# A tenth 2 MB home for expert weights, and half of each gather moved behind the pair's first unit

## The reference, cut to what matters

```
x = x + mixed @ w_out
h = rmsnorm(x, ln2)
logits = h @ w_router + b_router
top_v, top_i = top_k(logits, 4)            # 4 of 32 experts
gate = softmax(top_v)
for each expert e and its tokens:
    gu = h @ w_gate_up[e] + b_gate_up[e]   # 1024 x 2048
    gt, up = gu[:, :1024], gu[:, 1024:]
    gt = minimum(gt, 7); up = clip(up, -7, 7)
    y = ((up + 1) * gt * sigmoid(1.702 * gt)) @ w_down[e] + b_down[e]   # 1024 x 1024
    x = x + gate * y
y_prompt, y_sample = rmsnorm(x, ln_f)
```

## Time and profile before

| | |
|---|---|
| median of three runs | 1280.0 us (1279.75 to 1284.23) |
| the profiled execution | 1278.74 us, its span 1276.9 us |
| PE busy | 1204.8 us, 94% of the span |
| DVE, ACT, POOL busy | 27%, 16%, 7% |
| DMA | 458.76 MB, mean 359 GB/s |
| unit loads | 192 of 2 MB, 36 to 40 us from issue to landing |
| expert loop | 351.2 to 1266.1 us |

### The profile page before, as it was taken

How to read it: one execution, slowest core, us unless ns; L and a number is a source line. 1 busy time by engine, 2 the same in 40 slices (tenths; PEclk the granted TensorE clock), 3 DMA queues, 4 the chain that set the end, 5 groups by cost and what they waited for, 6 DMA issues and landing times.

```text
span 1276.9 us, 18583 instructions
## 1 busy us (share of the span) xinstructions
PE 1204.8 (94%) x7592; PEld 590.1 (46%) x7592; DVE 339.3 (27%) x655; ACT 208.3 (16%) x421; POOL 87.0 (7%) x64
## 2 busy tenths in 40 slices
PE   6999999999999999999998989999898989898997
PEld 5877789875543433434333333324242433333332
DVE  1068497566411111111111111011111111111102
ACT  3133253320310110111011001000110101010002
POOL 0161003711000000000000000000000000000001
PEclk9999999999999999999999999999999999999999
DMA  9879450158699999999999999999999999999994
GB/s 318 196 249 300 141 210 12 37 191 339 272 379 428 428 427 429 428 426 428 428 429 425 429 428 427 427 428 429 427 428 428 428 428 428 427 428 427 428 427 185
DMA packets 52656, 458.76 MB, mean 359 GB/s; under 512 B 7092, under 2 KB 10844, under 8 KB 28004
## 3 DMA queue, kind: packets, MB, share of 16 engines
q1 hardware_dynamic: 49972, 452.22, 86.2%
q0 software_dynamic: 1824, 5.12, 1.7%
q10 hardware_dynamic: 784, 0.28, 0.1%
HBM read 453.74 MB, written 3.82 MB: 358 GB/s over the span
## 4 chain that ended last, share of the span: by engine, by line
PE 60%; DMA 29%; DVE 6%; ACT 2%; POOL 1%; issue 1%; SPq 0%; DVEq 0%; ACTq 0%; POOLq 0%
DMA ring<-in_w_gate_up 29%; PE ps L1902 24%; PE ps L1409 8%; PE ps L1923 7%; PE ps L1835 6%; PE ps L1882 3%; PE ps L1740 2%; PE ps L1844 2%; DVE work L904 2%; PE ps L1911 1%; DVE ring L904 1%; PE ps L1385 1%; PE ps L1727 1%; DVE ring L949 1%; PE ps L1657 1%
## 5 line engine op out<-in xcount | busy, mean ns | idle before, releaser
L1902 PE MATMUL ps<-ring,work 128*64 128x512 f32 x1456 | 326.5, 596 | 32.8 <-DMA ring<-in_w_gate_up 30.8
L1902 PEld LDWEIGHTS ps<-ring,work 128*64 128x64 f32 x1456 | 100.9, 137 | 236.9 <-issue 190.7
L1299 DVE TENSOR_SCALAR work<-ps 128x512 f32<-128x512 f32 x32 | 22.1, 692 | 529.0 <-PE ps L1902 529.0
L1409 PE MATMUL ps<-work,ring 128*128 128x264 f32 x672 | 156.4, 392 | 2.3 <-ACT work L552 2.2
L1902 PE MATMUL ps<-work 128*64 128x512 f32 x592 | 132.7, 594 | 11.6 <-DMA work<-in_w_gate_up 11.6
L1409 PEld LDWEIGHTS ps<-work,ring 128*128 128x128 f32 x672 | 127.5, 192 | 28.1 <-issue 6.2
L1923 PE MATMUL ps<-ring,work 128*64 128x512 f32 x608 | 137.3, 597 | 0.0
L1923 PE MATMUL ps<-work 128*64 128x512 f32 x416 | 93.3, 593 | 0.6 <-DMA work<-in_w_down 0.6
L1317 DVE SCALAR_TENSOR_TENSOR work<-work 128x512 f32<-128x512 f32 x32 | 24.0, 752 | 240.9 <-ACT work L775 240.9
L1902 PEld LDWEIGHTS ps<-work 128*64 128x64 f32 x592 | 42.4, 137 | 95.2 <-issue 88.9
L1923 PEld LDWEIGHTS ps<-ring,work 128*64 128x64 f32 x608 | 41.2, 137 | 92.7 <-issue 90.5
(11 more groups left out here) (276 smaller groups left out, 889.8 us busy)
## 6 DMA issues: line engine op xcount, KB each, us to landing
ring<-in_w_gate_up SPq DMA_DIRECT2D x91, 2048.0 KB, 36.3
ring<-in_w_down SPq DMA_DIRECT2D x38, 2048.0 KB, 40.1
work<-in_w_gate_up SPq DMA_DIRECT2D x37, 2048.0 KB, 36.8
work<-in_w_down SPq DMA_DIRECT2D x26, 2048.0 KB, 39.2
ring<-in_w_in SPq DMA_DIRECT2D x5, 3072.0 KB, 16.4
ring<-in_w_out SPq DMA_DIRECT2D x1, 4096.0 KB, 14.1
ring<-in_w_in SPq DMA_DIRECT2D x2, 1536.0 KB, 9.0
ring<-in_cache_k SPq DMA_DIRECT2D x16, 192.0 KB, 7.5
```

What stands on the lines that cost most here:

```text
L1299: v.tensor_scalar(gt, PS[BG][:, :], LIMIT, None, ALU.min).then_inc(S_("gt"), 1)
L1409: last_ = mm(psum(job, T), w, hT[:, k, :], start=k == 0, stop=k == KD - 1)
L1902: last = mm(PS[bnk][g * 64:g * 64 + 64, :], lhs, UNIT[n % 9][:, w0 + base + g * 512:w0 + base + (g + 1) * 512], start=False, stop=k == KD - 1)
```

## The change

1. **Ten homes.** `HOMES` is 10; a home of 4096 columns at `WORK` 520 joins. It lies over constants that only the first part needs, over small tensors and old state. So the constants are re-ordered, the ones needed late first; two of them are stored narrower, and `before` is loaded later, next to the router, at another place. `acc` moves to `WORK` 4616, small late tensors to 17352.
2. **Releases.** Units 3 and 4 are released at the fourth step of the `mb` products (behind the wait for `obT` 4), units 5 and 6 after `mb7` ahead of the sample's output projection, 7 and 8 after `wo10` and `wo11`, 9 with `open_sum(1, 1)`.
3. **Residual input.** It is loaded into `h2`, by POOL, after `obT` 4 and after all seven stores of `st_out`, the state's among them. `residual` adds PSUM and `h2` into `acc`.
4. **One `XG`.** `gather(0)` of the next pair moves from behind `combine` to k = 4 of the second expert, and `gather(1)` of the pair itself comes at k = 2 of its first expert, into bank BY. `act_T` moves to k = 2 of the second expert. DVE builds the next `sel` after that `gather(1)`.
5. **Small loads.** `ebias` is laid out over 128 partitions and loaded after `ht21`; `ln_f` is loaded by SP behind the last unit, when unit 182 has been used.
6. **Loops.** PE's loop holds all 16 pairs, SP's five pairs a turn. Some semaphores are merged.

```diff
-        UNIT = [view(RING, 4096 * 5, 4096), view(RING, 4096 * 2, 4096), view(RING, 4096 * 3, 4096), view(RING, 4096 * 4, 4096),
-                view(WORK, 13256, 4096), view(WORK, 24504, 4096), view(RING, 0, 4096), view(RING, 4096, 4096),
-                view(WORK, 2792, 4096)]
+        UNIT = [view(RING, 4096 * 5, 4096), view(RING, 4096 * 2, 4096), view(RING, 4096 * 3, 4096), view(WORK, KEPT, 4096),
+                view(WORK, 13256, 4096), view(RING, 4096 * 4, 4096), view(WORK, 24504, 4096), view(RING, 0, 4096),
+                view(RING, 4096, 4096), view(WORK, 4616, 4096)]
...
-            for m in range(2):
-                load(acc[:, m, :], A["x_prompt"][0, m * 128:(m + 1) * 128, :], "ld_acc")
-            load(acc[:NB, 2, :], A["x_sample"][:, 0, :], "ld_acc")
...
+            sp.wait_ge(S_("unit_used"), sp.snap(passes * (6 * NE) + (HOMES + 183 - 6 * NE)))
+            load(lnfb, A["ln_f"].unsqueeze(0).broadcast_to([128, D]), "ld_lnf")
...
+            pool.wait_ge(S_("obT"), 4)
+            pool.wait_ge(S_("st_out"), 16 * 7)
+            for m in range(2):
+                load(h2[:, m, :], A["x_prompt"][0, m * 128:(m + 1) * 128, :], "ld_acc")
+            load(h2[:NB, 2, :], A["x_sample"][:, 0, :], "ld_acc")
             pool.wait_ge(S_("mix"), KD)
             load(ln2b, A["ln2"].broadcast_to([128, D]), "ld_ln2")
+            load(C["before"], A["c_mats"][:, EARLY:EARLY + 128], "ld_router")
...
-            pool.wait_ge(S_("xgT_out"), 1)
-            load(lnfb, A["ln_f"].unsqueeze(0).broadcast_to([128, D]), "ld_lnf")
+            pool.wait_ge(full[bank["ht21"]], turn["ht21"])
+            for i in range(2):
+                for g in range(2):
+                    load(ebias[(2 * i + g) * NE:(2 * i + g + 1) * NE, :], A["b_gate_up"][0, :, i * FE + g * 512:i * FE + (g + 1) * 512], "ld_ebias")
...
                 if c == 2:
                     after(pe, "ma7")
                     pe.sem_inc(S_("unit_used"), 1)
+                if c == 3:
+                    pe.sem_inc(S_("unit_used"), 2)
...
             out_projection(0, 0)
+            after(pe, "mb7")
+            pe.sem_inc(S_("unit_used"), 2)
             give("wo2")
...
-            after(pe, "ma7", "mb7")
-            pe.sem_inc(S_("unit_used"), 3)
...
-            gather(0)
-            bank_free(BY)
-            gather(1, BY)
+            gather(0, BX)
             pe.wait_ge(S_("samp_out"), 1)
             first_bias(1)
-            pe.wait_ge(S_("xgT_out"), 1)
+            bank_free(BY)
             pe.wait_ge(S_("gate"), 3)
...
                 for k in range(KD):
+                    if e_ and k == 2:
+                        act_T(pr * 2 + 1)
                     if e_ and k == 4:
                         pe.wait_ge(S_("actT_out"), pr * 2 + 2)
-                        gather(1)
+                        pe.wait_ge(S_("sel_next"), pr * 4 + 4)
+                        gather(0, BX)
+                    if e_ == 0 and k == 2:
+                        pe.wait_ge(S_("y_out"), pr * 2 + 1)
+                        gather(1, BY)
                     if e_ == 0 and k % 4 == 0:
                         pe.wait_ge(S_("xgT_out"), pr * 2 + 1 + k // 4)
...
-                pe.wait_ge(S_("sel_next"), pr * 4 + 4)
-                pe.wait_ge(S_("actT_out"), pr * 2 + 1)
-                gather(0)
-                pe.wait_ge(S_("up"), pr * 2 + 1)
-                bias(pr * 2 + 2, pick_e[1])
-                pe.wait_ge(S_("xgT_out"), pr * 2 + 3)
-                act_T(pr * 2 + 1)
                 pe.wait_ge(S_("selg"), pr * 4 + 4)
                 for n in range(4):
                     last = nc.tensor.transpose(PS[BY][:, n * 128:(n + 1) * 128], selg_e[n // 2][:, n % 2, :], C["ident"])
                 last.then_inc(S_("selgT_full"), 1)
+                pe.wait_ge(S_("up"), pr * 2 + 1)
+                bias(pr * 2 + 2, pick_e[1])
```

More of the change, by code:

```diff
@@ L164, in bc @@
             return ap.broadcast_to(shape)
-        mats = view(WORK, 0, len(CONST_NAMES), 128)
-        C = {n: mats[:, i, :] for i, n in enumerate(CONST_NAMES)}
-        sm = [128 * len(CONST_NAMES)]
+        starts = [sum(w for _, w in CONSTS[:i]) for i in range(len(CONSTS))]
+        C = {n: view(WORK, at, w) for (n, w), at in zip(CONSTS, starts)}
+        C["before"] = view(WORK, 24320, 128)
+        assert starts[5] == KEPT and starts[-1] == EARLY
+        sm = [EARLY]
         def small(*dims):
@@ L196, in build @@
         mcount = small(1)
-        thr = small(PASSES)
-        marks = small(PASSES)
         qkvT = view(WORK, 2792, CA, T)
@@ L402, in _ @@
             load_win(0, "b")
-            load(WORK[:, 128:128 * len(CONST_NAMES)], A["c_mats"][:, 128:], "ld_mats")
+            load(WORK[:, 128:EARLY], A["c_mats"][:, 128:EARLY], "ld_mats")
             load_win(1)
@@ L737, in _, with gathered @@
             route_exp(2)
-            def gathered(P, half, count, b=BX):
+            def gathered(half, count, b):
                 act.wait_ge(S_("xg_full"), count)
-                nc.scalar.activation(XG[P % 2][:, half, :, :, OWN:SLOT],
+                nc.scalar.activation(XG[:, half, :, :, OWN:SLOT],
                                      PS[b][:, :].rearrange("p (c e s) -> p c e s", c=4, e=2)[:, :, :, OWN:SLOT], ACT.Copy)\
@@ L777, in _ @@
             with act.Fori(0, passes) as p:
-                with act.Fori(0, NE // 4) as four:
-                    for q in range(2):
-                        pr = act.snap(p * (NE // 2) + four * 2 + q)
-                        sigmoid(pr * 2)
-                        gathered(q + 1, 0, pr * 2 + 3)
-                        act_transposed(pr * 2)
-                        act.wait_ge(S_("selgT_full"), pr + 1)
-                        nc.scalar.activation(selgT_e[0], PS[BY][:, 0:256], ACT.Copy)
-                        nc.scalar.activation(selgT_e[1], PS[BY][:, 256:512], ACT.Copy).then_inc(S_("selgT_out"), 1)
-                        gathered(q + 1, 1, pr * 2 + 4)
-                        sigmoid(pr * 2 + 1)
-                        expert_rows(pr * 2, pr * 12 + 19)
-                        act_transposed(pr * 2 + 1)
-                        expert_rows(pr * 2 + 1, pr * 12 + 21)
-            A_(nc.scalar.activation(lss[:1], eps[:1], ACT.Sqrt))
+                with act.Fori(0, NE // 2) as pair:
+                    pr = act.snap(p * (NE // 2) + pair)
+                    gathered(1, pr * 2 + 2, BY)
+                    sigmoid(pr * 2)
+                    act.wait_ge(S_("selgT_full"), pr + 1)
+                    nc.scalar.activation(selgT_e[0], PS[BY][:, 0:256], ACT.Copy)
+                    nc.scalar.activation(selgT_e[1], PS[BY][:, 256:512], ACT.Copy).then_inc(S_("selgT_out"), 1)
+                    act_transposed(pr * 2)
+                    gathered(0, pr * 2 + 3, BX)
+                    sigmoid(pr * 2 + 1)
+                    expert_rows(pr * 2, pr * 12 + 20)
+                    act_transposed(pr * 2 + 1)
+                    expert_rows(pr * 2 + 1, pr * 12 + 22)
+            A_(nc.scalar.activation(lss2[:1], eps2[:1], ACT.Sqrt))
             for m in range(2):
@@ L927, in _ @@
             V.free(tt(biasS[:64], psum("bvs", NKEY, parts=64), log_s[:64], ALU.add), "bvs")
-            V.ready(v.memset(mcount, 0.0), "bvec", 1)
+            V.ready(v.memset(mcount, 0.0), "rows_out", 1)
             def score(h):
@@ L1830, in _, with gather @@
             done(mm(rk[:, 2, :], C["ones"], selr[:, 1, :], start=False, stop=True), "rk")
-            def gather(half, b=BX):
+            def gather(half, b):
                 for c in range(4):
@@ L1922, in down @@
                         w0 = (k % 4) * 1024 + g * 512
-                        last = mm(PS[BY][g * 64:g * 64 + 64, :], lhs, UNIT[n % 9][:, w0:w0 + 512], start=k == 0, stop=k == KD - 1)
+                        last = mm(PS[BY][g * 64:g * 64 + 64, :], lhs, UNIT[n % HOMES][:, w0:w0 + 512], start=k == 0, stop=k == KD - 1)
                     if k % 4 == 3:
@@ L1954, in _ @@
             with pe.Fori(0, passes) as p:
-                with pe.Fori(0, 2) as t:
-                    landed = [pe.snap(p * 352 + t * 128), pe.snap(p * 336 + t * 128)]
-                    for i in range(6):
-                        expert_pair(i, pe.snap(p * 16 + t * 6 + i), landed)
-                landed = [pe.snap(p * 352 + 256), pe.snap(p * 336 + 256)]
-                for i in range(4):
-                    expert_pair(i, pe.snap(p * 16 + 12 + i), landed)
+                landed = [pe.snap(p * 320), pe.snap(p * 304)]
+                for i in range(NE // 2):
+                    expert_pair(i, pe.snap(p * (NE // 2) + i), landed)
             end = pe.snap(passes * NE)
```

168 lines of the change are left out of this document (87 added, 81 removed).

## The result

The changed kernel takes 1289.0 us, the median of ten runs (1283.6 to 1295.3); the kernel before takes 1279.9 us beside it (1278.1 to 1289.2). The ratio of the two sets of runs is put at 1.0052, 95% interval 1.0034 to 1.0069; the two medians alone are 9.2 us or 0.7% apart. The forecast was 1272.4, range 1270.5 to 1278.0: wrong in sign, and outside its range. The profiled execution took 1289.7 us, its span 1287.9 us, 11.0 more than before.

A forecast was written before the change was run, and what follows sets the result against it. The prediction took the weight stream over DMA, 428 GB/s, and its start to bound the kernel. Gains of 4.94 + 1.65 + 1.0 = 7.6 us against the median of 1280.0 gave 1272.4 us, range 1270.5 to 1278.

The forecast's parts named there:

- the inputs of the residual: Before the second norm: inputs moved to POOL's queue land near 303.5 us, ln_2 near 311.5; cost 0.
- the third rival: Before the second norm: store's small parts each wait for a unit; 4.3 us slower, 1284.3, up to 1290; chance 0.07.
- The row: Small loads beside the stream: each 4 KB row waits behind one 8 KB unit row, 0.31 + 0.15 us.
- the rule that stood beside the step: DMA queues: an engine drains some 9 to 17 descriptors from one ring first, so small loads may wait for a unit's share.
- The store: Before the residual inputs: the state's store, issued at 278.65 us, takes 14.2 us and lands at 292.9.
- The first rival: Before the second norm: small loads wait for whole units, 2.2 us of PE idle, 1274.6 us; chance 0.17.
- The tenth home: Expert loop: ten units landed at the first release instead of nine, one less follows; 4.94 us gained.
- the holes: Before the first release: idle DMA time has room for the extra unit, with 12 us to spare.
- The gather: Loop start and end: moving gathers behind the first unit gains 1.65 us at the start and 1.0 at the end.
- The second release: Early expert loop: it comes 5.6 us after the first, leaving a DMA hole of 0.7 us; all but 0.2 cancels.
- ln_f: End of the stream: queued behind unit 191, it lands about 1257 us, before its reader at 1262; cost nothing.
- edits with one answer: Memory moves, merged semaphores, extra memset, biases in row groups, fewer early constants and unrolled loops: 0 us.

The follow-up runs named there:

- quarters: The changed kernel with units 0 to 6 each loaded by four transfers of 512 KB, 1024 columns each (4 KB rows): 1277.4 us, ratio 0.9967.
- halves_of_short_rows: The changed kernel with units 0 to 6 each in two transfers of 1 MB, each taking every second 4 KB piece of a row: 1275.8 us, ratio 0.9963.
- store_by_sp: The changed kernel with the state's store issued by SyncE right behind the output weight instead of by ScalarE: 1278.1 us, ratio 0.998.
- after_again: The changed kernel measured once more, nothing changed: 1289.4 us.
- units_in_halves: The changed kernel with units 0 to 6 each in two transfers of 1 MB by columns, 8 KB a row: 1276.0 us, ratio 0.995.
- inputs_by_sp: store_by_sp with the residual inputs and ln_2 also issued by SyncE in its own queue, between early units: 1273.6 us in five runs, ratio 0.9948.
- before_again: The kernel before the change measured once more, nothing changed: 1281.0 us.
- nine_homes: inputs_by_sp with nine homes instead of ten, ln_f at another place and SP's loop taking three pairs a turn: 1279.9 us, ratio 0.9983.

## Why the prediction was wrong, step by step

**The step that failed is the one on the inputs of the residual, costed at 0.** It had two mis-sized terms, and it was the third rival that came nearest. What the runs showed in its place: the inputs landed at 325.5 us and `ln_2` at 331.4, not at 303.5 and 311.5 (some 6 us of it by the late early part), and PE stood 8.8 us, as each row of a small load waits for one 16 KB row of the stream.

*The row.* The sum put each 4 KB row of a small load behind "one 8 KB row of a unit (0.31 + 0.15 us)". The row is 16 KB, as two rows of `w_gate_up` or four of `w_down` lie side by side in memory for each partition. The packets of SP's queue count it: 49812 after, 52836 with seven units in quarters. The difference is 3024 = 7 x (512 - 128) rows and 21 more transfers x 16. Rows of 8 KB would have given 7 x (512 - 256) and the same 336, so 2128. With 16 KB the price is 0.61 + 0.15 = 0.77 us a row. The service one by one, which the step assumed, then fits what the runs show. An engine has 8 rows of each half of `x_prompt`, so their mean landing (the median of two is their mean) is at (8 + 16)/2 = 12 rows plus something fixed. The quarters give that: 8.1 us less 12 x 0.31 = 3.7, so 4.4 us.

| row | us a row | x_prompt by this | measured |
|---|---|---|---|
| 4 KB | 0.31 | 8.1 (fitted) | 8.1 (quarters), 8.5 (halves_of_short_rows) |
| 8 KB | 0.46 | 9.9 | 9.8 |
| 16 KB | 0.77 | 13.6 | 13.2, 13.2 (after twice), 13.6 (store_by_sp) |
| 16 KB at half rate (32 partitions) | 1.38 | 21.0 | 21.8 |

`x_sample` has one row on an engine and is behind them in the queue. Served one by one it lands 5 rows after that mean, 3.8 us; if an engine served eight rows of a unit at a turn, it would be half of a whole unit's 4.9 us plus a small half unit (3.1) later, 8.0 us. DVE, which waited for nothing else, began 4.8 us after the mean (after: 307.2 + 0.3 + 13.2 = 320.7, DVE at 325.54), and 4.7 in `after_again` and in `store_by_sp`. With 32 partitions the two are 6.9 and over 15, and 6.7 was measured.

This also decides between the trace and the rule that stood beside the step. The Trainium skill, DMA: Bandwidth & Descriptors, "Queues, rings and completion order", has an engine drain some 9 to 17 descriptors before it turns to another ring. With two transfers of 1 MB in rows of 4 KB, sixteen rows on an engine could go in one such turn, and the small loads would wait as with 8 KB rows; they waited as with quarters. And the rows counted above are decisive: on an engine they alternate, one of each queue in every 0.6 us, where a turn of eight rows of a unit alone would last 4.9 us. For these queues the trace shows turns of one row.

Had the rows been the 8 KB that the sum assumed, it would have held: in `units_in_halves` the inputs landed at 312.7 us and `ln_2` at 319.8, DVE waited for none of them, and PE had no idle time at the norm.

*The store.* The sum took the 14.2 us of the earlier trace rows over, though its surroundings changed: before, short input loads stood between `w_out` and the units, and unit 0 was fetched later. The rows by queue show it. The store has 528 of them, 33 an engine. Before, 490 had gone by 288.4 us, beside 4 KB rows, and only 38 went beside units. In the changed kernel 176 had gone by 291.6, and the other 352, 22 an engine, took 15.5 us beside 16 KB rows. From issue to landing 22.2 and 19.3 us were measured, and 14.5 with rows of 8 KB. The third rival said just that, "lands near 305, the inputs near 322 and ln_2 near 328", with a price of 11.9 us of idle PE. They landed at 307.1, 325.5 and 331.4 in a run whose early part was 6 us late, and PE stood 8.8 us. The prediction had given it 0.07. Its mechanism is right but for one word: each short row waits for a row of a unit, not for a unit. That the measured 1289.0 also lies within its "up to 1290" is partly luck, as that time holds a late early part that the rival doesn't know. What was held against it, that units were already there for half of the 14.2 us, was the wrong comparison: the units stood beside the last third of that time, and beside a tenth of the rows.

*What follows the idle time* wasn't in the third rival: 1.8 us for a clock of 0.50 to 0.81 after it.

**The first rival** (small loads wait for whole units, 1274.6) has the size right by another mechanism: in `store_by_sp` the inputs took 18.5 us where its terms add up to 17.1 (its landing at 312.5 makes 18.2 of them), and 0.9 us of PE idle passed on where it said 2.2.

**The tenth home: right.** 4.94 forecast; the loop's length gives 4.8. The full gain in the loop is 5.4 in the profile after, 5.8 to 6.1 in `store_by_sp` and `inputs_by_sp` (919.9 and 919.6 for 925.7) where 5.9 was forecast. It fits in the holes, DMA stays at 428, and unit 189 binds at the end, as worked out.

**The gather: mechanism right, size wrong by the profiles.** 1.65 + 1.0 forecast, 0.7 + 0.4 between two profiles, 2.8 between the medians. The transpose came when it was to come; the entry of the loop took 0.85 us of it back. The second release left no more of a hole than before: DMA is short of 428 by 2.5 us in the 42 us after the first release in `inputs_by_sp`, and by 2.2 before.

**ln_f and the edits with one answer: right.** `ln_f` took 39.6 us behind the last unit and nobody waited.

**The part ahead** wasn't in the sum: the constants' new order seemed to cost nothing, and PE doesn't wait for them. But a few tenths decide whether DVE and POOL meet, and the meeting near 96 us is worth some 4 us in a single execution (marks of 153.5 to 155.4 without it, of 157.9 to 159.6 with it). It widens any range that is drawn for this kernel.

Put together, as an estimate: with the measured 22.2 us for the store, the fixed 4.4 us and 0.77 us a row, the step's own working gives the store landed at 300.9 (278.65 + 22.2), the inputs 17.5 us later (17 x 0.77 + 4.4) at 318.4, `ln_2` 6.1 us on at 324.5, and PE idle from 317.8 to 325.8. These 8.0 us and the 1.8 of the clock, less 5.9 and 0.7, are 3.2 us slower, 1283.2. From `w_out` on the profiles give 4.7 us (after and before) and 3.0 (`after_again` and `before_again`). The 9.2 us between the medians also hold the early part, which was 6.1 and 5.4 us later in the two profiles of the changed kernel.

## What to carry to other kernels

On each DMA engine every row of a small load waited for one row of the stream beside it: count the load's rows, find the length of the stream's rows by the packets in the profile, and don't carry a landing time over to other surroundings. Put small loads in the stream's own queue ahead of it, or cut the few large transfers that they meet into shorter rows. Before an issue is made to wait for another engine's store, ask when that store will land once the change has moved the stream beside it.

## What the hardware showed that was not expected

- Two queues with work took turns of one row on each DMA engine: 65 rows of the stream and 65 of the store in 2.4 us, 162 and 162 in 7.0 us beside the inputs.
- Rows of 16, 8 and 4 KB in the stream gave a 512 KB load 13.2, 9.8 and 8.1 to 8.5 us in another queue, at the same rate of the stream.
- A transfer into 32 partitions kept all 16 DMA engines busy at 216 to 230 GB/s, half of the 428.
- VectorE's `tensor_scalar` of 0.35 us took up to 3.6 us beside a GpSimd product of 3.4 us, and `scalar_tensor_tensor` with two SBUF inputs up to 3.7.
- After 8.8 us without a matmul TensorE's clock was granted at 0.50 and cost 1.8 us. In two profiles (`nine_homes`, `after_again`) the loop's first 16 records took 5.35 us instead of 3.65, too.
- PE stands 0.85 to 0.95 us when it enters a loop with no matmuls queued ahead of it, for nothing that the profile names.
